# A two-layer mixer and a mixer/MLP block on one core: gates evicted at other units, the sink inside the maximum, a fourth slot for one high part, unit-matrix products beside the last sums

## What is computed

```python
def first_block(x, ...):
    for layer in range(2):
        h = rmsnorm(x, norm_g[layer])
        # layer 0: a gated convolution (a) beside block attention (b)
        # layer 1: three-branch attention (c) beside banded attention with sinks (d)
        y = concatenate([y_left * silu(z_left), y_right * silu(z_right)])
        x = x + y @ w_out[layer]
    return x

def masked_softmax(s, mask, sink=None):
    m = max(s, axis=-1)
    if sink is not None:
        m = maximum(m, sink)
    e = where(mask, exp(s - m), 0)
    den = sum(e, axis=-1)
    if sink is not None:
        den = den + exp(sink - m)
    return e / maximum(den, TINY)

def second_block(x, c, ...):
    # retention and dilated attention, gated and merged, then a squared-ReLU MLP
    x = x + g1 * token_mixer(modulate(rms_norm(x, g_1), ...))
    x = x + g2 * square(relu(modulate(rms_norm(x, g_2), ...) @ w1)) @ w2
    return rms_norm(x, g_f)
```

## Time and profile before

| | us |
|---|---|
| median of three runs | 884.95 |
| lowest, highest | 884.6, 885.35 |
| the profiled execution, its own time | 884.18 |
| its span, first to last instruction | 882.4 |
| mean granted TensorE clock (1 is 2.4 GHz) | 0.996 |

### The profile page before, as it was taken

One profiled execution on the slowest core, in us unless ns is written; L12 is line 12 of the kernel. 1 busy time (PEld: TensorE's weight loads), 2 busy tenths in 40 slices (PEclk: granted clock), 3 DMA queues, 4 the chain that ended last, 5 costly groups with the idle time before them and its releaser, 6 DMA issues.

```text
span 882.4 us, 17028 instructions
## 1 busy us (share of the span) xinstructions
PE 863.6 (98%) x6944; PEld 817.8 (93%) x6944; DVE 408.9 (46%) x1015; ACT 468.2 (53%) x706; POOL 674.2 (76%) x552
## 2 busy tenths in 40 slices
PE   7999999999989999999999999999999999999997
PEld 6899899998879999889997899999999999999997
DVE  3899745635785576953554223321124642210001
ACT  4545766377876623344444565875336665534431
POOL 0987549748935799798767787678899899987880
PEclk9999999999999999999999999999999999999998
DMA  8855586884210597876575444545546555545521
GB/s 324 339 186 198 204 292 226 307 313 144 87 59 2 205 408 261 344 276 242 195 268 181 166 144 148 188 143 192 191 147 246 191 186 188 189 144 191 192 96 48
DMA packets 28484, 177.62 MB, mean 201 GB/s; under 512 B 3144, under 2 KB 5844, under 8 KB 8056
## 3 DMA queue, kind: packets, MB, share of 16 engines
q1 hardware_dynamic: 27112, 174.87, 54.0%
q10 hardware_dynamic: 1296, 1.68, 0.6%
HBM read 174.95 MB, written 3.43 MB: 202 GB/s over the span
## 4 chain that ended last, share of the span: by engine, by line
PE 95%; DVE 2%; ACT 1%; issue 1%; POOL 1%; DMA 1%; POOLq 0%; SPq 0%; DVEq 0%; ACTq 0%
PE proj L793 20%; PE proj L795 19%; PE proj L796 19%; PE proj L829 4%; PE proj L874 3%; PE proj L872 3%; PE proj L875 3%; PE mixed L1021 1%; PE scores L976 1%; PE transposed L990 1%; PE proj L1074 1%; PE proj L1143 1%; PE mixed L1004 1%; PE scores L963 1%; PE proj L1077 1%; PE proj L1076 1%
## 5 line engine op out<-in xcount | busy, mean ns | idle before, releaser
L695 POOL TENSOR_TENSOR w_lo<-raw,w_hi 128x512 fp32r<-128x512 f32 x348 | 445.2, 1320 | 126.3 <-ACT w_hi L1434 126.3
L795 PE MATMUL proj<-parts,w_lo 128*128 128x256 f32 x1000 | 279.4, 279 | 0.6 <-POOL w_lo L695 0.6
L793 PE MATMUL proj<-parts,w_hi 128*128 128x256 f32 x952 | 270.3, 284 | 0.6 <-POOL w_lo L695 0.4
L796 PE MATMUL proj<-parts,w_hi 128*128 128x256 f32 x952 | 265.8, 279 | 0.0
L1434 ACT ACTIVATE w_hi<-raw 128x2048 fp32r<-128x2048 f32 x84 | 161.0, 1917 | 109.3 <-DMA raw<-in_weights 58.9
L795 PEld LDWEIGHTS proj<-parts,w_lo 128*128 128x128 f32 x1000 | 188.1, 188 | 1.7 <-POOL w_lo L695 0.8
L793 PEld LDWEIGHTS proj<-parts,w_hi 128*128 128x128 f32 x952 | 179.0, 188 | 3.4 <-issue 2.2
L796 PEld LDWEIGHTS proj<-parts,w_hi 128*128 128x128 f32 x952 | 179.0, 188 | 0.0
L695 POOL TENSOR_TENSOR w_lo<-arena,w_hi 128x512 fp32r<-128x512 f32 (+2 forms) x56 | 67.7, 1245 | 27.3 <-ACT w_hi L1434 27.3
L1446 ACT ACTIVATE arena<-proj 128x512 f32<-128x512 f32 x32 | 18.9, 597 | 53.2 <-PE proj L796 36.5
L872 PE MATMUL proj<-w_hi,parts 128*128 128x512 f32 x112 | 45.1, 403 | 0.0
(11 more groups left out here) (448 smaller groups left out, 2157.0 us busy)
## 6 DMA issues: line engine op xcount, KB each, us to landing
raw<-in_weights SPq DMA_DIRECT2D x106, 1024.0 KB, 5.0
arena<-in_weights SPq DMA_DIRECT2D x31, 1024.0 KB, 7.6
wide<-in_weights SPq DMA_DIRECT2D x9, 1024.0 KB, 6.9
probT<-in_weights SPq DMA_DIRECT2D x8, 1024.0 KB, 5.0
dil_lines<-dil_line SPq DMA_DIRECT2D x1, 2304.0 KB, 12.3
prob<-in_weights SPq DMA_DIRECT2D x2, 1024.0 KB, 4.8
dil_bias<-dil_lines SPq DMA_DIRECT2D x1, 1536.0 KB, 9.8
xT<-in_x SPq DMA_DIRECT2D x4, 256.0 KB, 5.6
```

Source lines behind the costliest of these rows:

```text
L695: nc.gpsimd.tensor_tensor(lo_slots[RAW_AT[n]][:, at], raw_slots[RAW_AT[n]][:, at], hi_slots[HI_AT[m]][:, at].bitcast(F32), ALU.subtract).t ...
L793: nc.tensor.matmul(dst, whi, h, start=first, stop=False)
L795: nc.tensor.matmul(dst, wlo, h, start=False, stop=False)
L796: last = nc.tensor.matmul(dst, whi, lo[:, k, :], start=False, stop=stop)
```

## The change

Four edits, independent of each other:

1. **Gates at other units.** In `FILL_CD` the evictions of zc0 and zc1 stand one unit later, that of zd1 one unit earlier, and the first `scale_bias` of d goes behind unit 3 instead of unit 2.
2. **The sink in the maximum.** The d scores' maximum starts from the sink instead of -3e38, so that it holds the sink; three small DVE instructions per d unit and one at the start go. ACT takes four exponentials of 128x1, each of sink minus maximum, in place of one of 128x4.
3. **A fourth slot.** `wo0_3`'s high part goes into the slot `w_hi_b`; the units behind it take the slots of their predecessors.
4. **Unit-matrix products.** PE runs three 128x128 products of the unit matrix with itself behind the first of the last column sums, and three behind the last, into a bank that nobody reads.

```diff
 FILL_CD = [x.split() for x in (
-    "S: N:kd E:zc0", "zc1.0 E:kd", "zc1.1", "E:zc1", "modA zd0.0.0", "zd0.0.1 E:modA", "",
-    "zd0.1", "zd1.0 E:zd0", "", "zd1.1.0", "zd1.1.1", "L:y0", "H:0 E:zd1 L:y1", "H:1", "")]
-SCALE_BEFORE, SCALE_BEHIND = {6: (0, 1), 12: (1, 1)}, {2: (0, 0), 7: (1, 0)}
+    "S: N:kd", "zc1.0 E:zc0 E:kd", "zc1.1", "", "E:zc1 modA zd0.0.0", "zd0.0.1 E:modA", "",
+    "zd0.1", "zd1.0 E:zd0", "", "zd1.1.0", "zd1.1.1", "E:zd1 L:y0", "H:0 L:y1", "H:1", "")]
+SCALE_BEFORE, SCALE_BEHIND = {6: (0, 1), 12: (1, 1)}, {3: (0, 0), 7: (1, 0)}
...
-HI_AT, HI_BEFORE = take_slots(SPLIT, lambda n, u: [*range(NHI), NHI + 1] if u in SHARED_HI else range(NHI + sum(n >= SPLIT_AT[start] for start in HI_MORE)))
+HI_AT, HI_BEFORE = take_slots(SPLIT, lambda n, u: [NHI + 1] if u == "wo0_3" else [*range(NHI), NHI + 1] if u in SHARED_HI else range(NHI + sum(n >= SPLIT_AT[start] for start in HI_MORE)))
...
+        def sink_of(at, i):
+            f, b = divmod(i, 2)
+            return sinks[:, 2 * at + b + 4 * f:][:, 0:1]
...
+            def keep_running(n):
+                for _ in range(n):
+                    nc.tensor.matmul(pt[:, 0:P], ident, ident, start=True, stop=True)
...
                     column_sums(0, True, False)
+            keep_running(3)
             pe.wait_ge(stream_sq, squares_of("xf", KD - 1))
             column_sums(KD - 1, False, True).then_inc(norm_sum, 1)
             state["norm"] += 1
+            keep_running(3)
             stream_spread("xf")
             stream_spread("xf", sc[0], sem("second_spread"))
...
+                    elif v == "wo0_3":
+                        act.wait_ge(sem("line_ready"), 1)
...
-                if part == "d":
-                    last = nc.scalar.activation(s[:, 12:16], s[:, 12:16], ACT.Exp)
+                for i in range(4) if part == "d" else ():
+                    last = nc.scalar.activation(s[:, 12 + i:13 + i], sink_of(at, i), ACT.Exp, bias=s[:, 4 + i:5 + i])
...
-                                                     scale=q_rstd[:, "bcd".index(part), at, i8:i8 + 1], scalar=-3e38,
+                                                     scale=q_rstd[:, "bcd".index(part), at, i8:i8 + 1],
+                                                     scalar=sink_of(at, i) if part == "d" else -3e38,
...
-                sk, down = (cut(v[:], 4)[:, :, 2 * at:2 * at + 2] for v in (sinks, no_sinks))
-                own.did(V.tensor_tensor(cut(top, 2), cut(top, 2), down, ALU.min))
-                own.settle()
-                own.did(V.tensor_copy(s[:, 4:8], top))
-                V.tensor_tensor(cut(s[:, 12:16], 2), cut(top, 2), sk, ALU.add).then_inc(mx_ready, 1)
...
-            own.did(V.tensor_scalar(no_sinks, sinks, -1.0, None, ALU.mult))
```

More of the change, by code:

```diff
@@ L2007, in score_max @@
                 top = st[:, S + 12 + 4 * (u % 3):S + 12 + 4 * (u % 3) + 4]
[L2008 removed]
+                own.did(V.tensor_reduce(top, e[:, :, 0:n], AX.X, ALU.max, negate=True))
                 own.settle()
[L2010 to L2017 removed]
+                V.tensor_scalar(s[:, 4:8], top, 1e28, None, ALU.min).then_inc(mx_ready, 1)
             def normalise(u):
```

11 lines of the change are left out of this document (3 added, 8 removed).

## The result

| | before | changed |
|---|---|---|
| median, 21 executions each (us) | 884.95 | 885.95 |
| lowest, highest | 883.67, 886.66 | 885.03, 887.14 |
| ratio of the two | | 1.0013 (1.0007 to 1.0019) |
| the profiled execution, its own time | 884.18 | 885.41 |
| its span | 882.4 | 883.6 |

The forecast was 885.5 with a range of 882.7 to 887.8 and "no change that a measurement can tell" as the likeliest class. The time lies in the range and in that class, 0.45 us above the forecast. So the sum held. The executions of the changed kernel lie in two groups, ten with a mean clock of 1.000 at 885.03 to 885.87 and eleven with 0.998 or 0.999 at 885.95 to 887.14; the profiled one is of the first, and what the second loses is not shown.

What follows compares the result with a forecast made beforehand. PE, busy 98% of the span, bounds the kernel, so only its waits and clock count. 0.64 + 0.0 + 2.33 - 1.45 - 0.93 = +0.6 us on the median of 884.95 gave 885.5 us, range 882.7 to 887.8.

Steps and rivals of the forecast that it cites:

- no change that a measurement can tell: Whole kernel: time between 883.2 and 886.7 us, chance 0.60; about 0.2%, 1.8 us, is what a measurement can tell.
- slot of wo0_3: First output product: two PE waits for the low part go (1.01 us), a new 1.65 us stall comes; net +0.64 us.
- zc0 later: Units 1 and 2: one PE wait takes the other's place; 0.0 us, bounds -0.3 to +0.2.
- zc1 and scale_bias: Behind unit 3: both ACT steps queue behind its copies, delaying DVE's gate and unit 6's maximum; +2.33 us.
- sink and zd1: Units 12 and 13: PE's waits of 1.18 and 0.83 us shrink or go; -1.45 us, bounds -0.5 to -2.0.
- end, to the last instruction: Last two spreads: unit products keep PE's clock full, POOL's last piece and the store behind it come earlier; -0.93 us.
- stall at the third piece: First output product: the wo0_3 copy ahead of the operand's third piece on ACT makes PE stall 1.65 us.
- zd0 at +1.25: Behind unit 3: zd0.0.0 needs bank 0 and begins at about 227.95 instead of 226.70, 1.25 us later.
- unit 6's transposes at +2.33: Behind zd0: PE's transposes of unit 6 come 2.33 us later, since DVE has no idle stretch to catch up.
- the moved steps are harmless: Rival, whole kernel: ACT and DVE absorb the moved work; together 5 us down, 880; chance 12% with its half.
- the stall behind unit 4 decides: Rival: that stall costs 2.3 to 2.6 us, units 12 and 13 gain only 0.55, the end nothing; 887.4, chance 22%.
- the 0.55 us: Unit 12, DVE between maximum and copy: three instructions leave, the most PE's 1.18 us wait ahead of its transposes can lose.

Runs made afterwards that it cites:

- e1: The changed kernel with the gate of zc1 and the first scale_bias put back where they stood before; 884.05 us, 0.9994 of before.
- e10: e1 with wo0_3's high part copied into its own slot behind the operand's fourth piece instead of ahead of the third; 882.18 us, 0.997 of before.
- e5: The kernel before with only the gate of zd1 one unit earlier; 883.92 us, ratio 0.9987.
- e9: The kernel before with only the six unit-matrix products of the end; 884.69 us, ratio 0.9996 (0.9987 to 1.0005).
- e3: The changed kernel with wo0_3's high part in the shared slot again; 886.55 us, ratio 1.0024.
- e15: The kernel before with only the sink in the maximum; run once for its trace, 103.45 us from 167 to 271 us against 103.89 before.
- e4: The changed kernel without the six unit-matrix products of the end; 886.89 us, ratio 1.0021.

## Why the prediction was right, and where its steps were not

| step | forecast | measured in the traces |
|---|---|---|
| slot of wo0_3 | +0.64 | +0.1 to +0.2 |
| zc0 later | 0.0 | -0.04 |
| zc1 and scale_bias | +2.33 | +2.30 |
| sink and zd1 | -1.45 | -1.00 |
| end, to the last instruction | -0.93 | -0.55 (-0.92 to POOL) |
| sum | +0.6 | +0.8 to +0.9, and +1.0 in the median |

**Right, by its own steps.** The stall at the third piece (1.65 us forecast, 1.54 to 1.64 measured), zd0 at +1.25 and unit 6's transposes at +2.33 (+1.24 and +2.31 measured, changed against e1), found by going forward from the row that can't move, and the 0.0 of zc0. The rival "the moved steps are harmless" is refuted by e1 and e10: each of the two new stalls is real and takes off what it was said to. The rival "the stall behind unit 4 decides" had the mechanism right too, but its condition failed: the gate of zd1 at its earlier unit holds PE by 0.15 us and no more (e5), and all that the sink and zd1 win is 1.0 us, not 0.55.

**The slot's gain was mis-sized**, 1.01 us for two waits. Removed without a new stall (e10) they gave 1.44. The 1.01 was the sum of the numbers in brackets, and these begin only where the modelled 0.28 us of the last product end, while PE starts one every 0.117 us. By starts, and their neighbours show it:

```profile
133.77 0.28 PE L796 MATMUL proj<-parts,w_hi 128*128 128x256 f32 x1
...
135.90 0.28 PE L793 MATMUL proj<-parts,w_hi 128*128 128x256 f32 x1
```

From 133.77 to 134.42 it is 0.65 us in place of 0.12, and from 135.90 to 136.82 it is 0.92: 1.33 us, and the product behind each wait takes about 0.1 more.

**The step of the sink and zd1 was mis-sized twice.** It took the 0.55 us from the reduction to the copy as the whole, though the copy still has to follow the reduction, and it priced the new start value of the maximum at nothing: 0.33 came. And it had POOL's low part arrive just when PE wants it: it comes 0.25 us late, and 0.67 came in place of 0.90. For that place the prediction looked at ACT's exponentials of unit 12 alone, which are covered; those of unit 13 are not. They took 0.65 us more in place of the 0.3 taken. The Trainium skill, "Perfetto Trace Analysis", section "Optimizing Scalar/DVE Operations", gives ScalarE about 93 ns of data access for each instruction on SBUF and about twice that in a profile; by this four tiny ones come near four times one, and the trace agrees, with 0.85 against 0.21.

**The end's step failed at one sentence**: that DVE's quarters end ahead of POOL "and so do not become the bound". They do end ahead, but their stores fill the transfers' time up to POOL's own. And the clock falls at another moment in each execution, as the prediction weighed: from the start of the first spread on, in it, in the second, or behind both. The Trainium skill, "TensorE: Matmul & The Clock Gate", section "What's actually happening", speaks of windows that run freely; the five traces without products agree with it. The prediction made of it half of the gain for the median, and still put the whole 0.93 into its sum. Of the median no run tells the share: e9's interval takes in both nothing and the whole.

Against the profiled execution the forecast came out 0.2 to 0.3 us low: 0.45 from the sink and zd1 and 0.4 from the end, less 0.45 to 0.55 from the slot. That the slot's error stands against the others is chance. Against the median it was 0.45 us low; with the end's gain of the five traces, 0.1 us on the mean, in place of the 0.55 the steps add up to about 1.3 us, and the measured 1.0 has an interval of 0.6 to 1.7.

## What to carry to other kernels

A step moved to where its engine looks idle is late for whoever waits for that engine next; go forward from a row that can't move, through every step queued behind it, and ask the same of a copy that moves up because its buffer is free: here one `break` in the order turned a loss of 0.2 us into a gain of 1.4. Price a wait by the distance from start to start, not by the idle time in brackets. At the end of a kernel, find what the transfers of the output have been doing since the first one began, before crediting the last engine. And take a second trace before pricing a fall of the clock: the one here was the worst of five.

## What the runs showed of the hardware

- In e3 one stall of PE of 0.81 us was followed by 3.4 us at a granted clock of 0.50, and both cost 2.3 us. By the waits in its trace it came from a single small transfer inside the chip that landed after 9.2 us, where the middle of the four took 5.3.
- A maximum fused with a bias takes 0.54 us for 128x256 values with its start value from a column, and 0.48 with a constant (changed kernel and e15 against the one before).
- PE's last product ends at 878.50 in e4, and the clock falls 0.8 us behind it; with the unit products ahead of the spreads it fell 4.3 us behind PE's last product in the changed kernel, 4.1 in e1 and 3.7 in e9.
- The four stores at the end, 1.05 MB, ran at 350 to 400 GB/s without a gap, and the end stood 5.33 to 5.41 us behind the start of DVE's first quarter in the changed kernel, the one before, e4, e5 and e9.
